# Down-projection of a decoder step: plain 32-bit matmuls with the weights held whole, in place of three split products in two column passes

## The reference, cut to what matters

```python
x = x + concat[gdn heads, dsa heads] @ w_out
[g, u] = causal_depthwise_conv3(RMSNorm(x) @ w_up) + b
y = x + (silu(g) * u) @ w_down            # (2056 x 2816) @ (2816 x 1024)
```

## Time and profile before

| | us |
|---|---|
| median of 3 runs (4825.85 to 4834.21) | 4829.94 |
| the profiled execution | 4815.95 |
| its span, first to last instruction | 4814.7 |
| PE (TensorE matmul) busy in the span | 4014.5 |
| PEld (TensorE weight load) busy | 3209.8 |
| DVE (VectorE) / ACT (ScalarE) / POOL (GpSimd) busy | 2131.5 / 1490.0 / 706.9 |

### The profile page before, as it was taken

How to read it: one execution, slowest core, us unless ns; L and a number is a source line. 1 busy time by engine, 2 the same in 40 slices (tenths; PEclk the granted TensorE clock), 3 DMA queues, 4 the chain that set the end, 5 groups by cost and what they waited for, 6 DMA issues and landing times. The chain is left out here.

```text
span 4814.7 us, 51474 instructions
## 1 busy us (share of the span) xinstructions
PE 4014.5 (83%) x19226; PEld 3209.8 (67%) x19290; DVE 2131.5 (44%) x4175; ACT 1490.0 (31%) x2357; POOL 706.9 (15%) x564
## 2 busy tenths in 40 slices
PE   6768686878757888898877825998999999979999
PEld 4434354544426877777766824448999999968877
DVE  1155898889872443343232272223344344431200
ACT  1102565556542444444431200112222222221211
POOL 0010000000002322222110002111111111114433
PEclk8879898989875898998885555999999999989999
DMA  2033121211013111111013002321111111135433
GB/s 64 26 106 101 43 64 48 63 35 59 24 51 106 45 36 37 38 31 40 12 30 123 35 1 88 105 88 37 53 53 35 53 53 35 53 118 175 131 106 114
DMA packets 285863, 302.47 MB, mean 63 GB/s; under 512 B 33652, under 2 KB 230420, under 8 KB 279383
## 3 DMA queue, kind: packets, MB, share of 16 engines
q1 hardware_dynamic: 270170, 256.80, 18.4%
q10 hardware_dynamic: 13408, 22.44, 1.4%
q0 software_dynamic: 2112, 20.97, 1.2%
HBM read 206.35 MB, written 94.10 MB: 62 GB/s over the span
## 5 line engine op out<-in xcount | busy, mean ns | idle before, releaser
L552 PE MATMUL chan_p_g<-ht,chan_w 128*128 128x412 f32 (+1 forms) x1920 | 730.0, 526 | 35.8 <-ACT chan_flat L593 20.0
L1665 PE MATMUL up_p_g<-ht_high,up_wh 128*128 128x412 f32 (+1 forms) x1760 | 617.9, 351 | 0.1
L1665 PE MATMUL up_p_g<-ht_low,up_wh 128*128 128x412 f32 (+1 forms) x1760 | 615.9, 350 | 0.0
L1665 PE MATMUL up_p_g<-ht_high,up_wl 128*128 128x412 f32 (+1 forms) x1760 | 615.7, 350 | 0.0
L552 PEld LDWEIGHTS chan_p_g<-ht,chan_w 128*128 128x128 f32 x1920 | 375.0, 198 | 296.9 <-issue 241.6
L2065 ACT ACTIVATE chan_signed<-chan_sc,chan_trial 128x512 bf16<-128x512 f32 (+6 forms) x224 | 305.0, 1362 | 146.7 <-DVE chan_trial L2120 132.2
L1683 ACT ACTIVATE up_pre<-up_p_g 128x412 f32<-128x412 f32 (+1 forms) x220 | 113.3, 515 | 748.3 <-PE up_p_g L1665 748.3
L1665 PEld LDWEIGHTS up_p_g<-ht_high,up_wh 128*128 128x128 f32 x1760 | 331.8, 189 | 1.7 <-issue 0.5
L1665 PEld LDWEIGHTS up_p_g<-ht_low,up_wh 128*128 128x128 f32 x1760 | 331.5, 188 | 1.2
L1665 PEld LDWEIGHTS up_p_g<-ht_high,up_wl 128*128 128x128 f32 x1760 | 331.5, 188 | 0.4
L2106 DVE TENSOR_SCALAR_CACHE_REDUCE chan_tie<-chan_sc,chan_trial 128x384 bf16<-128x384 f32 (+6 forms) x224 | 316.1, 1411 | 7.6
(11 more groups left out here) (519 smaller groups left out, 6802.3 us busy)
## 6 DMA issues: line engine op xcount, KB each, us to landing
down_a<-scratch_act SPq DMA_DIRECT2D x88, 512.0 KB, 3.6
scratch_act<-up_acc SPq DMA_DIRECT2D x22, 1028.0 KB, 5.2
up_w<-in_w_up SPq DMA_DIRECT2D x44, 512.0 KB, 6.3
chan_iq<-scratch_iq SPq DMA_DIRECT2D x28, 512.0 KB, 7.2
scratch_qkv<-chan_acc SPq DMA_DIRECT2D x12, 1028.0 KB, 3.9
chan_w<-in_w_in SPq DMA_DIRECT2D x24, 512.0 KB, 4.1
mid_raw<-scratch_qkv SPq DMA_DIRECT2D x16, 768.0 KB, 5.4
proj_x<-in_x_prompt SPq DMA_DIRECT2D x16, 512.0 KB, 3.2
```

What stands on the lines that cost most here:

```text
L552: last = pe.matmul(p_g[at % BANKS][:, 0:cols.stop - cols.start], w[n % 2][:, k, :], K.ht[:, k, cols], start=(k == 0), stop=(k == KD - 1))
L1665: last = pe.matmul(p_g[u][:, 0:cols.stop - cols.start], wp[s][:, k, :], hp[:, k, cols], start=(k == 0 and m == 0), stop=(k == KD - 1 and m ...
```

## The change

Only `ffn_down` changes.

- The splits are gone: no `wh`, `wl`, `ah`, `al`, `sah`, `sal`, no work on ScalarE or GpSimd other than DMA issue, and one plain 32-bit matmul in place of three `F32R` ones.
- The weights are held whole and as they come: `w` of 22 x 1024 numbers per partition, fetched in 11 pieces of 1 MB issued at once by ScalarE's queue, with the samples' activations behind them.
- The outer loop over column halves is gone. A step fetches the same 512 KB of activations (ring of 5, freed by the matmuls of the step) and multiplies them with both halves: 2 blocks x 4 token tiles x 2 halves. There are 44 steps in place of 88.
- A group of 4 tiles fills all 8 banks. A bank is added to the residual as soon as it is finished (`s_done`), and the first matmul of the next group on it waits for that (`s_y`).
- Residual tiles are full rows of 1024, 6 of them; stores and later residual loads alternate in SyncE's program. The sample tile comes last, after all prompt tiles.

```diff
-        RING, BANKS = 3, 8
-        LAST = 2 * NGRP * CH
+        RING, XRING, BANKS = 5, 6, 8
+        LAST = NGRP * CH
...
+        w = c.sb("w", [P, NF, D])
+        a = ring("a", RING, [P, 2, WIDE])
+        sa = c.sb("sa", [P, NF, DEC])
+        x = ring("x", XRING, [P, D])
...
                 if t >= RING:
-                    sp.wait_ge(s_al, t - RING + 1)
...
+                    sp.wait_ge(s_mm, t - RING + 1)
+                sp.dma_start(a[t % RING][:, :, :], K.d_act[2 * k:2 * k + 2, :, g * WIDE:(g + 1) * WIDE].rearrange("f p n -> p f n"))\
+                  .then_inc(s_a[t % RING], 16)
...
+            for g in range(NGRP):
+                for k in range(CH):
+                    fetch(g * CH + k)
+                    if k == 6 and g == 0:
+                        for i in range(XRING):
+                            residual(i)
+                    if k == 6 and g:
+                        for i in range((g - 1) * TG, g * TG):
+                            store(i)
+                            if i + XRING < PER:
+                                residual(i + XRING)
+            for i in range((NGRP - 1) * TG, PER):
                 store(i)
+                if i + XRING < PER:
+                    residual(i + XRING)
...
+            for k in range(CH):
+                act.dma_start(w[:, 2 * k:2 * k + 2, :], rows[:, 2 * k:2 * k + 2, :]).then_inc(s_w[k], 16)
             act.dma_start(sa[:, :, :], K.d_act[:, :, SEQ:TOK].rearrange("f p n -> p f n")).then_inc(s_sa, 16)
...
         @block.tensor
         def _(pe):
+            for g in range(NGRP):
+                for k in range(CH):
+                    t = g * CH + k
+                    pe.wait_ge(s_a[t % RING], (t // RING + 1) * 16)
+                    if g == 0:
+                        pe.wait_ge(s_w[k], 16)
+                    for f in (2 * k, 2 * k + 1):
+                        for q in range(TG):
+                            for o in range(2):
+                                n = (g * TG + q) * 2 + o
+                                if f == 0 and n >= BANKS:
+                                    pe.wait_ge(s_y, n - BANKS + 1)
+                                last = pe.matmul(p_y[n % BANKS][:, :], a[t % RING][:, f % 2, q * P:(q + 1) * P], w[:, f, o * H:(o + 1) * H],
+                                                 start=(f == 0), stop=(f == NF - 1))
+                                if f == NF - 1 and n % BANKS < BANKS - 1:
+                                    last.then_inc(s_done, 1)
+                    last.then_inc(s_mm, 1)
+            pe.wait_ge(s_sa, 16)
             for o in range(2):
...
+                pe.wait_ge(s_y, NT * 2 - BANKS + o + 1)
+                for f in range(NF):
+                    last = pe.matmul(p_y[o][0:DEC, :], sa[:, f, :], w[:, f, o * H:(o + 1) * H], start=(f == 0), stop=(f == NF - 1))
+                last.then_inc(s_done, 1)
...
+            for i in range(PER):
+                rows, m = rows_of(i)
+                dve.wait_ge(s_x[i % XRING], (i // XRING + 1) * 16)
+                for o in range(2):
+                    n = i * 2 + o
+                    if i < NT and n % BANKS == BANKS - 1:
+                        dve.wait_ge(s_mm, (i // TG + 1) * CH)
+                    else:
+                        dve.wait_ge(s_done, n - n // BANKS + 1)
+                    part = x[i % XRING][0:m, o * H:(o + 1) * H]
+                    dve.tensor_tensor(part, p_y[n % BANKS][0:m, :], part, ALU.add).then_inc(s_y, 1)
```

More of the change, by code:

```diff
@@ L1759, in ffn_down @@
         PER = NT + 1
-        RING, BANKS = 3, 8
-        LAST = 2 * NGRP * CH
+        RING, XRING, BANKS = 5, 6, 8
+        LAST = NGRP * CH
         ring = lambda name, n, shape, dt=F32: [c.sb(f"{name}{b}", shape, dt) for b in range(n)]
[L1763 to L1768, removed]
+        w = c.sb("w", [P, NF, D])
+        a = ring("a", RING, [P, 2, WIDE])
+        sa = c.sb("sa", [P, NF, DEC])
+        x = ring("x", XRING, [P, D])
         p_y = [c.ps(f"y{b}", [P, H]) for b in range(BANKS)]
-        s_w, s_next = c.sems("w", RING), c.sems("next", CH)
+        s_w = c.sems("w", CH)
         s_a = c.sems("a", RING)
-        s_x, s_st = c.sems("x", BANKS), c.sems("st", BANKS)
-        s_wh, s_wl, s_ah, s_al, s_mm, s_y, s_sa, s_sah, s_sal = (
-            c.sem(n) for n in ("wh", "wl", "ah", "al", "mm", "y", "sa", "sah", "sal"))
+        s_x, s_st = c.sems("x", XRING), c.sems("st", XRING)
+        s_mm, s_done, s_y, s_sa = (c.sem(n) for n in ("mm", "done", "y", "sa"))
         block = open_block(nc, stack, c)
[L1776 to L1781, removed]
         def rows_of(i):
-            t = i % PER
-            return (slice(SEQ, TOK), DEC) if t == 0 else (slice((t - 1) * P, t * P), P)
-        cols_of = lambda i: slice(i // PER * H, (i // PER + 1) * H)
+            return (slice(SEQ, TOK), DEC) if i == NT else (slice(i * P, i * P + P), P)
         @block.sync
@@ L1807, in store @@
[L1807 to L1818, removed]
@@ L1819, in _ @@
-            for i in tiles(1, NGRP - 1):
+                sp.wait_ge(s_y, i * 2 + 2)
+                dst = outs["y_prompt"][rows, :] if n == P else outs["y_sample"]
+                sp.dma_start(dst, x[i % XRING][0:n, :]).then_inc(s_st[i % XRING], 16)
+            for g in range(NGRP):
[9 more added lines that the diff above has]
+                                residual(i + XRING)
@@ L1826, in _ @@
             rows = w_down.rearrange("(f p) n -> p f n", p=P)
[L1828 to L1850, removed]
-            act.dma_start(sa[:, :, :], K.d_act[:, :, SEQ:TOK].rearrange("f p n -> p f n")).then_inc(s_sa, 16)
[L1852 to L1878, removed]
+            for k in range(CH):
+                act.dma_start(w[:, 2 * k:2 * k + 2, :], rows[:, 2 * k:2 * k + 2, :]).then_inc(s_w[k], 16)
@@ L1880, in _ @@
+            act.dma_start(sa[:, :, :], K.d_act[:, :, SEQ:TOK].rearrange("f p n -> p f n")).then_inc(s_sa, 16)
         @block.tensor
         def _(pe):
-            for o in range(2):
[L1883 to L1905, removed]
@@ L1914, in add @@
-            def add(o, g):
-                dve.wait_ge(s_mm, step_of(o, g, CH - 1) + 1)
-                for i in tiles(o, g):
-                    n = rows_of(i)[1]
-                    dve.wait_ge(s_x[i % BANKS], (i // BANKS + 1) * 16)
-                    dve.tensor_tensor(x[i % BANKS][0:n, :], p_y[i % BANKS][0:n, :], x[i % BANKS][0:n, :], ALU.add).then_inc(s_y, 1)
-            for k in range(CH):
-                low(0, k)
-            for g in range(NGRP - 1):
-                add(0, g)
-            for k in range(CH - 3):
-                low(1, k)
@@ L1926, in _ @@
-            add(0, NGRP - 1)
-            for k in range(CH - 3, CH):
-                low(1, k)
-            for g in range(NGRP):
-                add(1, g)
+            for i in range(PER):
[9 more added lines that the diff above has]
+                    dve.tensor_tensor(part, p_y[n % BANKS][0:m, :], part, ALU.add).then_inc(s_y, 1)
```

17 lines of the change are left out of this document (5 added, 12 removed).

## The result

The changed kernel takes 4954.76 us (median of 4 runs, 4953.07 to 4959.07) against 4830.14 us before (4 runs): ratio 1.0263, 95% interval 1.0247 to 1.0278, or 124.6 us slower. The forecast was 4956. The profiled execution took 4955.28 us, its span 4954.0.

What follows compares the result with a forecast made beforehand. TensorE's matmul stream alone was taken to bound the phase. Start 4292.0 + 1.7 slow start + 641.8 matmuls + 0.3 drain + 0.7 addition + 5.0 store and end + 1.25 around the span gave 4942.7, 4956 us on the median; range 4940 to 4974.

Steps and rivals of the forecast that it cites:

- Price of a call: Down-projection matmuls: each plain call is two records 0.429 us apart, 0.858 us against 0.683 for three; 748 calls take 641.8 us.
- Rival (a): Down-projection matmuls: passes cost this phase's own 0.2277 us each, adding 39.5 us, time 4996; chance 5%.
- rival (c): Down-projection calls: a plain call runs as one record of 0.429 us instead of two, time 4635; chance 2%.
- Why a pass is cheaper: Matmul streams: three-product form loads an operand for each stream, plain form for every second; 0.2277 against 0.2145 us a pass.
- Start: Phase start: first matmul needs only unsplit first activations and weight piece 0, so begins at 4292, not 4296.34; gain 4 us.
- Rival (b): Phase start: first activations wait longer behind or beside 11 MB of weights, time 4960 to 4970; chance 9%.
- Slow start: First matmuls of the phase: about four at the 1.2 GHz pitch after idling, 1.7 us extra, once.
- Supply, queue, group edges: After the start: fetches, SyncE's waits for stores and bank additions at group edges all keep pace, cost nothing.
- End: Phase end: sample tile hides the prompt's last additions and stores, leaving 0.6 us drain, one 0.7 us addition, one store.
- Sum: Whole phase: +126.8 us on the profiled execution, from +130.9 matmuls, -4.3 start, about 0 for slow start and end.

Runs made afterwards that it cites:

- plain_halves: Kernel before, its structure and splits kept, but one plain 32-bit matmul on high tiles replaces the three F32R ones: 4975.20 us, ratio 1.0301.
- plain_samples_apart: plain_halves with the samples' calls taken out from between the full ones and set in a row, once per half: 4957.99 us, ratio 1.0267.
- half_columns: Changed kernel with each call cut into two of 256 columns, doubling calls and weight loads: 4958.76 us.
- weights_wait: Changed kernel with weight pieces 1 to 10 held back until the first activations have landed: 4951.74 us, ratio 1.0251.
- three_f32r: Changed kernel's loop with three F32R calls per block on one rounded pair of tiles, low parts left out, replacing the plain call: 4825.18 us, ratio 0.9991.

## Why the prediction was right

- **Price of a call.** 1496 records were forecast, 0.429 us apart; 1496 came, and the stretch of 644.30 us over 1496 is 0.4307 with the slow start in it. Type alone (plain_halves, plain_samples_apart) gives the loss. Rival (a), 0.455 us, and rival (c), 748 records, are out. The Trainium skill (FP8 and Floating Point Precision, TensorE Precision Notes) gives true 32-bit multiplication four passes, and the trace agrees: a call takes 0.858 us, 4 x 0.2145. Counting passes at the F32R pitch would have missed by 39.5 us, because a plain pass and an F32R pass are not the same price.
- **Why a pass is cheaper.** This reason failed, though no number of the sum hung on it; it stood only as an argument against rival (a). I put the 0.014 us by which an F32R record exceeds its 512 columns down to its loading an operand for every stream. bf16 records load one per stream too and take 0.216 us, and so do the records of half_columns, whose load is as long as an F32R one (0.19 us). The surplus goes with the F32R type. What in the engine makes it, no run here shows.
- **Start.** Forecast 8.5 us from the activations' issue to the first matmul, measured 9.0. Rival (b) wanted 12.5 or more and is out, but its cause is real: weights_wait shows that the weight pieces beside them cost 3.8 us of the 9.0.
- **Slow start.** The first five records were followed after 1.02, three times 0.85 and 0.51 us, the rest after 0.43: 1.9 us, forecast 1.7.
- **Supply, queue, group edges.** Nothing, as forecast: the waits of the profile after show TensorE waiting once, for the first activations. SyncE's waits for the landing of stores are there, none longer than 6.3 us (the forecast allowed for 6.5, four times per group), and stop nobody:

```profile
SPq L1791 <- DMA out_y_prompt<-down_x: 53.6, 11, 6.3
PE down_p_y L1837 <- DMA down_a<-scratch_act: 29.9, 1, 29.9
```

- **End.** From the last addition's start to the end of the span 5.2 us, forecast 5.7.
- **Sum.** Forecast +126.8 us in the phase, measured +127.3: +133.2 in the stream (forecast 130.9, with 1.7 of slow start and 0.3 of drain), -3.8 from the first weight fetch to the first matmul (forecast -4.3), -2.1 behind the last one. The parts agree and not only the sum. That the forecast on the median (4956) came so near also has luck in it: the two medians differ by 124.6, and the profiled executions reach this phase at times up to 22 us apart (4281.8 to 4303.7), through phases that nobody changed.

## What to carry to other kernels

Where TensorE is busy without a gap, count records and their pitch, per operand type, from a phase of the same kernel that already uses the type; the number of products in the source says little (one plain 32-bit call costs 26% more than three F32R ones here). Work taken off other engines paid nothing in this phase. If operands of different types or of very different loaded widths must be multiplied, do them in runs and not in turns.

## What the runs showed of the hardware that was not expected

- At 512 columns and the full clock a bf16 record takes 0.216 us and a plain 32-bit record (two streams) 0.429. An F32R record takes 0.227 us, also where the same square is loaded again (three_f32r), and 0.23 where 8 columns are loaded.
- Plain 32-bit records are held up around a change between loads of 128 and of 8 columns, 0.30 us per block with one such pair in it. bf16 records are too, by 0.09 us at each of the two changes (0.31 for 0.216). F32R records are not the earlier trace rows.
- Taking turns between F32R and bf16 costs what the faster bf16 records gain (0.68 us per three), and with 8-column loads more (0.85).
